# Keeping split weights in a scratch for the second half, in a kernel of one core

## The chip, the cores and the metric

The kernel runs on one core of a Trainium2 chip. The metric is the device time of one execution in microseconds, as the median of several runs. The profile comes from one further execution of the same program.

## The reference

One layer of a hybrid decoder on x of 2048 tokens by 1024, in float32:

```
h = rmsnorm(x, g_pre) * (1 + scale) + shift          # scale, shift, gate from c @ w_ada + b_ada
p = h @ w_in                                         # 1024 x 8704
y_pool = pool_mixer(a_in) * silu(a_g)                # windowed means
y_hgrn = hgrn2_mixer(b_q, b_f, b_i) * silu(b_g)      # gated linear recurrence
y_conv = short_conv_mixer(c_x, c_b, c_c) * silu(c_g) # three taps
y_diff = diff_attention(d_q, d_k, d_v) * silu(d_g)   # 4 heads, two maps each, causal
merged = sum over b of sigmoid(m_g[b]) * (y_b @ w_merge_b)
out = x + gate * rmsnorm(merged @ w_out, g_post)
```

## The kernel before, in words

**Products.** A float32 product is made of three float32r matmuls: each operand is split into a high part (its rounding) and a low part (the rest), and high by high, low by high and high by low are added in PSUM. The projection h @ w_in is done in two halves of 1024 tokens, each with 34 units of 256 output columns (`PAIR_COLS`). A unit is one 2 by 2 block product, and is computed with 7 block products instead of 8 (a Winograd scheme): `PRODUCTS` = 7 x 68 = 476, of which 238 belong to each half. A product is 4 blocks of depth (`KH`) by 3 matmuls of 128x512, 12 matmuls. The 7 left operands of a unit are weights w and sums of weights s; the 7 right ones are blocks of h and their sums t1 to t4.

**Slots.** Every engine runs its own instruction stream, written out by hand as a loop over slots n = 0 to 485. In slot n TensorE does product n into bank gb[n % 2]. ScalarE copies product n-1 out (`copy_out`, L918) or VectorE adds it to an output (`add_out`, L1207). ScalarE rounds the weights of product n+3 (`high`, L902), VectorE makes their low part (`low`, L1197), and GpSimd makes the four sums of weights of the next unit (L753 to L765). The split weights lie in a ring of four (`RING`), three ahead of use (`LEAD`). SyncE issues every DMA, in order, among them two 512 KB loads of weights for each unit (L366, L371). So each weight block is loaded, summed and split twice, once for each half of the tokens.

**The start.** TensorE transposes the 16 blocks of x of the first half into five banks. VectorE and ScalarE evict them as h (`evict`, L1238 and L962). Then ScalarE rounds the seven right operands (`high_h`, L975), and VectorE (operands 0, 2, 3, 6) and GpSimd (1, 4, 5, and the sum t3) make the low parts (`low_h` L1263, `low` L774). The right operands of the second half are kept in a scratch, loaded from slot 230 on and split in slots 233 to 242 (`CHANGE`).

**Attention and mixers** are laid into the slots beside the products. Attention of the first half of the tokens runs over slots 50 to 109, that of the second half over slots 284 to 354. A step of it on TensorE is `attention_ahead` (scores, L1694) and `attention_behind` (the turned-back output L1726, the product with v L1720, the transposes of the probabilities L1708). ScalarE does the exponentials (L988), VectorE the maxima (L1290), the combination (L1322) and the normalised output `on` (L1327). The mixers work in 16 blocks of 128 tokens, eight per half, with bases 12 or 12.5 slots apart from slots 130 and 372 on (`MIX_BASE`). A block's steps have offsets from -17 to +15 against its base, `mix_step(n, offset)`. Three consecutive blocks overlap.

**The end.** When the trunk is over, a second block of instructions, `merge_and_output`, multiplies by the merge weights and w_out.

## Time and profile before

| | |
|---|---|
| median of 3 runs | 2574.45 us (2573.1 to 2575.48) |
| the profiled execution's own time | 2568.26 us |
| its span | 2566.5 us |
| TensorE (matmul) busy | 2284.2 us, 89% |
| VectorE busy | 1689.7 us, 66% |
| ScalarE busy | 1259.9 us, 49% |
| GpSimd busy | 1093.9 us, 43% |
| mean granted TensorE clock | 0.962 |
| DMA | 350.85 MB, mean 137 GB/s |

The span runs from the first to the last instruction of the profiled execution. Busy shares are averages over stages that differ. The stages, as times from the start of the span, are: start to 62 us, then the products of the first half to 1012 us (plain to 236, with attention to about 600, with mixers to 960), those of the second half to 2065 us (plain to 1130, attention to about 1600, mixers after it), and the merge to the end. Matmuls are pipelined, so a busy TensorE is not a TensorE at its peak, and idle time of another engine costs nothing by itself.

### The profile page before, as it was taken

What the parts mean: (1) busy time and instruction counts of PE and PEld (TensorE: products, weight loads), DVE (VectorE), ACT (ScalarE), POOL (GpSimd) and SP (SyncE); (2) the same over time, 40 slices, a digit from 0 to 9 for tenths busy, and PEclk for the clock granted to TensorE, in tenths of its full rate; (3) what the DMA queues carried; (4) which work ended last, traced back from release to release, by engine and by line L of the source; (5) the groups of instructions that cost most, each with busy time, mean ns of one, the idle gap of its engine ahead of it and who ended that gap; (6) DMA issues with size and microseconds to landing.
All of it is one profiled execution on the core that took longest, in us unless ns stands there. A gap on an engine that the chain in (4) does not pass through costs nothing. (4 is left out here: it accounts for less than half of the span.)

```text
span 2566.5 us, 35701 instructions
## 1 busy us (share of the span) xinstructions
PE 2284.2 (89%) x11572; PEld 1859.2 (72%) x11572; DVE 1689.7 (66%) x2872; ACT 1259.9 (49%) x2634; POOL 1093.9 (43%) x883
## 2 busy tenths in 40 slices
PE   3599999999989999998999999999999965989898
PEld 2487777777767777776887888777777744767676
DVE  6776666658888785547777777588888735344442
ACT  3454555535554545445666666445555343434341
POOL 1513323225664654323334333366566425243343
PEclk6799999999999999999999999999999988999999
DMA  6467544334433436453424242343343266576582
GB/s 224 142 201 226 152 131 130 111 96 140 124 112 110 124 103 202 135 155 95 129 79 118 80 117 63 117 128 113 111 129 111 93 213 184 148 208 175 154 223 63
DMA packets 351328, 350.85 MB, mean 137 GB/s; under 512 B 25904, under 2 KB 277168, under 8 KB 350128
## 3 DMA queue, kind: packets, MB, share of 16 engines
q1 hardware_dynamic: 351152, 348.66, 46.0%
q8 instruction: 91, 1.49, 0.3%
q14 instruction: 85, 0.70, 0.1%
HBM read 242.15 MB, written 106.43 MB: 136 GB/s over the span
## 5 line engine op out<-in xcount | busy, mean ns | idle before, releaser
L1622 PE MATMUL gb<-h_hi,w_hi 128*128 128x512 f32 x1904 | 785.8, 413 | 89.1 <-DVE o L1207 53.5
L1624 PE MATMUL gb<-h_hi,w_lo 128*128 128x512 f32 x1904 | 756.3, 397 | 0.0
L1623 PE MATMUL gb<-h_lo,w_hi 128*128 128x512 f32 x1904 | 754.2, 396 | 0.0
L1197 DVE TENSOR_TENSOR w_lo<-w,w_hi 128x512 fp32r<-128x512 f32 x340 | 304.7, 898 | 298.9 <-ACT w_hi L902 298.0
L1622 PEld LDWEIGHTS gb<-h_hi,w_hi 128*128 128x128 f32 x1904 | 365.5, 192 | 175.6 <-issue 98.6
L1624 PEld LDWEIGHTS gb<-h_hi,w_lo 128*128 128x128 f32 x1904 | 364.1, 191 | 80.5
L1623 PEld LDWEIGHTS gb<-h_lo,w_hi 128*128 128x128 f32 x1904 | 366.0, 192 | 66.5
L988 ACT ACTIVATE C_prob<-C_sc,C_negm 128x512 f32<-128x512 f32 (+3 forms) x320 | 198.8, 623 | 270.4 <-DVE C_negm L1290 269.0
L781 POOL TENSOR_TENSOR C_prob<-C_prob,C_cf 128x512 f32<-128x512 f32 (+3 forms) x160 | 161.3, 1027 | 344.3 <-DVE C_cf L1312 330.0
L918 ACT ACTIVATE o<-gb 128x512 f32<-128x512 f32 x272 | 161.3, 593 | 268.5 <-PE gb L1624 255.5
L902 ACT ACTIVATE w_hi<-w 128x512 fp32r<-128x512 f32 x340 | 212.0, 625 | 100.1 <-PE gb L1624 98.9
L765 POOL TENSOR_TENSOR w<-w,s 128x512 f32<-128x512 f32 x68 | 91.1, 1339 | 287.0 <-DVE w_lo L1197 286.4
L753 POOL TENSOR_TENSOR s<-w 128x512 f32<-128x512 f32 x68 | 97.9, 1439 | 264.7 <-DMA w<-in_w_in_dram 251.7
L1207 DVE TENSOR_TENSOR o<-gb,o 128x512 f32<-128x512 f32 x204 | 139.8, 685 | 77.8 <-PE gb L1624 77.5
L1197 DVE TENSOR_TENSOR w_lo<-s,w_hi 128x512 fp32r<-128x512 f32 x136 | 117.2, 862 | 104.5 <-ACT w_hi L902 104.2
L1290 DVE TENSOR_REDUCE C_negm<-C_sc 128x1 f32<-128x512 f32 (+3 forms) x320 | 179.7, 601 | 4.7 <-PE C_sc L1697 2.7
L2168 PE MATMUL D_mb<-D_y_hi,D_wm_hi 128*128 128x512 f32 x320 | 131.2, 410 | 50.7 <-DVE D_gate L2041 31.3
L2000 POOL TENSOR_TENSOR D_gate<-D_gate 128x1024 f32<-128x1024 f32 x32 | 98.1, 3066 | 158.3 <-DVE D_gate L2041 158.3
L1694 PE MATMUL C_sc<-C_ks,C_qt 128*128 128x512 f32 (+3 forms) x320 | 123.2, 385 | 32.2 <-ACT C_prob L988 23.9
L1720 PE MATMUL C_ob<-C_v_tok,C_at 128*128 128x128 f32 x1088 | 149.3, 276 | 1.1 <-ACT C_at L1001 1.1
L1720 PEld LDWEIGHTS C_ob<-C_v_tok,C_at 128*128 128x128 f32 x1088 | 139.3, 191 | 12.9 <-ACT C_at L1001 6.8
L1322 DVE SCALAR_TENSOR_TENSOR C_prob<-C_prob,C_cf 128x512 f32<-128x512 f32 (+3 forms) x160 | 144.5, 903 | 2.6 <-POOL C_prob L781 2.2
(231 smaller groups left out, 4118.2 us busy)
## 6 DMA issues: line engine op xcount, KB each, us to landing
w<-in_w_in_dram SPq DMA_DIRECT2D x136, 512.0 KB, 4.1
gT_scratch<-o SPq DMA_DIRECT2D x128, 256.0 KB, 2.8
D_gate<-gT_scratch SPq DMA_DIRECT2D x32, 1024.0 KB, 9.8
pT_scratch<-o SPq DMA_DIRECT2D x80, 256.0 KB, 2.9
C_qt<-qB_scratch SPq DMA_DIRECT2D x128, 128.0 KB, 2.9
C_ks<-kT_scratch SPq DMA_DIRECT2D x48, 256.0 KB, 4.8
A_x_all<-in_x_dram SPq DMA_DIRECT2D x16, 512.0 KB, 6.9
A_ada<-in_w_ada_dram SPq DMA_DIRECT2D x8, 1024.0 KB, 12.1
```

The costliest lines, as they stand in the source:

```text
L781: tt(second, second, cf[i % 3][:, 1, p:p + 1].to_broadcast([P, width(z)]), ALU.mult).then_inc(scaled, 1)
L902: a(w_hi[n % RING][:, :, :], source(n), ACT.Copy).then_inc(whi, 1)
L918: a(o[b][:, :], gb[n % 2][:, :], ACT.Copy).then_inc(copied, 1)
L988: a(prob[z % PROBS][:, m, 0:width(z)], sc[(2 * z + m) % 3][:, 0:width(z)], ACT.Exp, bias=negm[i % 2][:, m, p:p + 1], accum_out=sums[i % 2] ...
L1197: tt(w_lo[n % RING][:, :, :], source(n), w_hi[n % RING][:, :, :].bitcast(F32), ALU.subtract).then_inc(wlo, 1)
L1207: tt(o[b][:, :], gb[n % 2][:, :], o[c][:, :], ALU.add).then_inc(summed, 1)
L1290: nc.vector.tensor_reduce(negm[i % 2][:, m, p:p + 1], sc[(2 * z + m) % 3][:, 0:width(z)], AX.X, ALU.max, negate=True).then_inc(max_ready, 1)
L1322: stt(first_map, first_map, cf[i % 3][:, 0, p:p + 1], prob[z % PROBS][:, 1, 0:width(z)], ALU.mult, ALU.add).then_inc(a_ready, 1)
L1622: mm(to, hi[:, k, :], h_hi[j][:, k, :], start=(fresh and k == 0), stop=False, skip_group_check=True)
L1623: mm(to, hi[:, k, :], h_lo[j][:, k, :], start=False, stop=False, skip_group_check=True)
L1624: last = mm(to, lo[:, k, :], h_hi[j][:, k, :], start=False, stop=(k == KH - 1), skip_group_check=True)
L1720: last = mm(ob[i % 2][:, 0, :], at[z % 2][:, y, :], v_tok[:, 4 * p + y, :], start=(z == begin[i] and y == 0), stop=(p == 0 and y == nb - 1))
```

## The change

In the first half ScalarE, besides splitting the weights of each product, stores both parts (high and low, now one tensor `w_both` of 512 KB) to a DRAM scratch `wS`: `store_weights(n)`, issued from ScalarE's own DMA queue, two slots ahead of the product, after VectorE has made the low part. `high` waits for the store that last read its place in the ring. For the second half's 238 products `load_weights(n)` brings both parts back, three slots ahead, in place of the loads of w_in, the sums by GpSimd, `high` and `low`. TensorE waits for that load.

In the start the evictions are shared anew: ScalarE takes blocks 0 to 3 and 8 to 15, VectorE 4 to 7. All low parts and t3 of the first half are made by VectorE, with operand 5 ahead of 4.

The mixers' steps are placed anew: ScalarE's `sigmoids` is cut in three (`pool_sigmoid`, `sigmoids`, `affine` a slot later), `distances_x` in two steps each, `decays_first` in two, and several steps are one slot later. In the first half's attention `turn_back` is put behind `values` and `turn`.

The diff, cut to its core ("..." marks lines left out; the arithmetic of counts for the new order is left out whole):

```
@@ -139,8 +148,8 @@
...
-        w_hi = [sb(f"w_hi{j}", [P, KH, P], F32R) for j in range(RING)]
-        w_lo = [sb(f"w_lo{j}", [P, KH, P], F32R) for j in range(RING)]
+        w_both = [sb(f"w_both{j}", [P, 2, KH, P], F32R) for j in range(RING)]
+        w_hi, w_lo = [b[:, 0, :, :] for b in w_both], [b[:, 1, :, :] for b in w_both]
@@ -241,6 +250,9 @@
...
+        w_kept = [sem(f"w_kept{j}") for j in range(RING)]
+        KEEPS = [len(range(r, KEPT, RING)) for r in range(RING)]
@@ -624,9 +652,9 @@
...
-                if j == 1 and u + 1 < UNITS:
+                if j == 1 and u + 1 < NU:
                     load_w1(u + 1)
-                if j == 4 and u + 2 < UNITS:
+                if j == 4 and u + 2 < NU:
                     load_w2(u + 2)
@@ -837,19 +865,10 @@
...
-            for kk in range(2):
-                low(1, kk, 0, operand_part(1, kk))
-            for kk in range(2):
-                t3(0, kk)
-            for j in LOW_BY_POOL[1:]:
-                for kk in range(2):
-                    if j == 4:
-                        pool.wait_ge(t3_made, kk + 1)
-                    low(j, kk, 0, operand_part(j, kk))
...
-                if u + 1 < UNITS:
+                if u + 1 < NU:
@@ -893,6 +912,7 @@
...
                     act.wait_ge(product_done, n - RING + 1)
+                    act.wait_ge(w_kept[n % RING], 16 * (n // RING))
@@ -900,6 +920,17 @@
...
+            def store_weights(n):
+                act.wait_ge(wlo, n + 1)
+                act.dma_start(wS[n], w_both[n % RING][:, :, :, :].bitcast(F32).rearrange("p l k c -> p (l k c)")).then_inc(w_kept[n % RING], 16)
+            def load_weights(n):
+                act.wait_ge(product_done, n - RING + 1)
+                if n < KEPT + RING:
+                    act.wait_ge(w_kept[n % RING], 16 * KEEPS[n % RING])
+                act.dma_start(w_both[n % RING][:, :, :, :].bitcast(F32).rearrange("p l k c -> p (l k c)"), wS[n - KEPT]).then_inc(w_kept[n % RING], 16)
@@ -1034,11 +1060,18 @@
                     act.wait_ge(r_done, 4 * i - 4)
                     act.wait_ge(kt_ready, i - 1)
                 a(f_s[:, :, :], in3[i % 2][:, 2:4, :], ACT.Sigmoid)
-                link(a(k_s[i % 2][:, :, :], in3[i % 2][:, 2:4, :], ACT.Sigmoid, scale=-1.0))
+                a(k_s[i % 2][:, :, :], in3[i % 2][:, 2:4, :], ACT.Sigmoid, scale=-1.0)
+                link(a(q_s[i % 2][:, :, :], in3[i % 2][:, 0:2, :], ACT.Sigmoid))
+            def affine(i):
                 for t in range(2):
                     a(f_s[:, t, :], f_s[:, t, :], ACT.Identity, scale=omlb[:, t:t + 1], bias=lb[:, t:t + 1])
-                    a(k_s[i % 2][:, t, :], k_s[i % 2][:, t, :], ACT.Copy, scale=omlb[:, t:t + 1])
-                a(q_s[i % 2][:, :, :], in3[i % 2][:, 0:2, :], ACT.Sigmoid).then_inc(sig_ready, 1)
+                for t in range(2):
+                    ins = a(k_s[i % 2][:, t, :], k_s[i % 2][:, t, :], ACT.Copy, scale=omlb[:, t:t + 1])
+                ins.then_inc(sig_ready, 1)
+            def pool_sigmoid(i):
                 act.wait_ge(a_loaded, 32 * (i + 1))
                 if i >= 2:
                     act.wait_ge(yp_ready, i - 1)
@@ -1087,26 +1120,32 @@
                 root_x(0, t)
             for n in range(LEAD):
                 high(n)
-            for kk in range(2):
-                high_h(0, kk)
-            for q in range(4, 8):
+            act.wait_ge(mod_ready, 1)
+            for q in range(4):
                 evict(0, q)
-            for kk in range(2):
-                high_h(1, kk)
-            for q in range(12, 16):
+            for j in range(2):
+                for kk in range(2):
+                    high_h(j, kk)
+            for q in range(8, 16):
                 evict(0, q)
             for kk in range(2):
                 high_h(2, kk)
+            for n in range(LEAD - 1):
+                store_weights(n)
             for n in range(SLOTS):
                 u, j = divmod(n, PER)
                 if n and n - 1 < PRODUCTS and (n - 1) % PER in COPIED:
                     copy_out(n - 1)
-                if n + LEAD < PRODUCTS:
+                if n + LEAD - 1 < KEPT:
+                    store_weights(n + LEAD - 1)
+                if n + LEAD < KEPT:
                     high(n + LEAD)
+                elif n + LEAD < PRODUCTS:
+                    load_weights(n + LEAD)
                 if n < 4:
                     for kk in range(2):
-                        high_h(3 + n, kk)
+                        high_h(FIRST_ORDER[3 + n], kk)
                 for b, off in OUT_SLOT.items():
                     for late in range(2):
                         v, r = divmod(n - off - late, PER)
@@ -1168,11 +1211,11 @@
...
-                for t, off in enumerate((-5, -2)):
+                for t, off in enumerate((-5, -1)):
...
-                i = mix_step(n, -1)
+                i = mix_step(n, 0)
@@ -1246,20 +1288,24 @@
...
+            def t3_first(kk):
...
+                tt(parts(h12, kk), parts(h22, kk), parts(h12, kk), ALU.subtract).then_inc(t3_made, 1)
@@ -1359,15 +1405,18 @@
...
-            def distances_x(i, t):
+            def distances_x(i, t, y0, y1):
...
-                for y, m in enumerate(LEVELS):
+                for y in range(y0, y1):
+                    m = LEVELS[y]
...
+                if y1 < NL - 1:
+                    return
@@ -1381,10 +1430,12 @@
...
-            def decays_first(i):
+            def decay_first_queries(i):
...
+            def decay_first_keys(i):
@@ -1457,12 +1508,11 @@
...
-            for q in range(4):
+            for q in range(4, 8):
...
-            for kk in range(2):
-                low_h(0, kk, 0, operand_part(0, kk))
-            for q in range(8, 12):
-                evict(0, q)
+            for j in range(2):
+                for kk in range(2):
+                    low_h(j, kk, 0, operand_part(j, kk))
@@ -1473,17 +1523,18 @@
             for n in range(SLOTS):
                 if n and n - 1 < PRODUCTS and (n - 1) % PER in SUMMED:
                     add_out(n - 1)
-                if n + LEAD < PRODUCTS:
+                if n + LEAD < KEPT:
                     low(n + LEAD)
                 if n == 0:
                     for kk in range(2):
-                        low_h(3, kk, 0, operand_part(3, kk))
-                if n == 1:
+                        t3_first(kk)
+                if n == 2:
                     for kk in range(2):
                         t4(0, kk)
-                if n == 3:
+                if n < 4:
+                    j = FIRST_ORDER[3 + n]
                     for kk in range(2):
-                        low_h(6, kk, 0, operand_part(6, kk))
+                        low_h(j, kk, 0, operand_part(j, kk))
                 for b, off in OUT_SLOT.items():
                     v, r = divmod(n - off, PER)
                     if r == 0 and 0 <= v < UNITS and kind(v) in ("q", "k", "gate"):
@@ -1566,26 +1617,35 @@
                 i = mix_step(n, -8)
                 if i is not None:
                     scan(i)
+                i = mix_step(n, -7)
+                if i is not None:
+                    distances_x(i, 0, 0, 3)
                 i = mix_step(n, -6)
                 if i is not None:
-                    distances_x(i, 0)
+                    distances_x(i, 0, 3, NL - 1)
                 i = mix_step(n, -5)
                 if i is not None:
                     decay_keys(i)
                 i = mix_step(n, -4)
                 if i is not None:
-                    decays_first(i)
+                    decay_first_queries(i)
                 i = mix_step(n, -3)
                 if i is not None:
-                    distances_x(i, 1)
-                i = mix_step(n, 10)
+                    decay_first_keys(i)
+                    distances_x(i, 1, 0, 2)
+                i = mix_step(n, -2)
+                if i is not None:
+                    distances_x(i, 1, 2, NL - 1)
+                i = mix_step(n, 11)
                 if i is not None:
                     advance_state(i)
+                i = mix_step(n, 12)
+                if i is not None:
                     pool_out(i)
                 i = mix_step(n, 14)
                 if i is not None:
                     finish(i)
-                i = mix_step(n, 0)
+                i = mix_step(n, 1)
                 if i is not None:
                     decay_queries(i)
@@ -1604,15 +1664,15 @@
...
-                else:
...
+                pe.wait_ge(*lo_count(half, j, 1))
...
-                    pe.wait_ge(wlo, n + 1)
+                    if n < KEPT:
+                        pe.wait_ge(wlo, n + 1)
+                    else:
+                        pe.wait_ge(w_kept[n % RING], 16 * (KEEPS[n % RING] + (n - KEPT) // RING + 1))
@@ -1734,15 +1788,15 @@
                     turn_back(i)
             def attention_behind(half, s):
-                i = None if half else finished(half, s, ON)
-                if i is not None:
-                    turn_back(i)
                 z = piece(half, s, VALUES)
                 if z is not None:
                     values(z)
                 z = piece(half, s, TURN)
                 if z is not None:
                     turn(z)
+                i = None if half else finished(half, s, ON)
+                if i is not None:
+                    turn_back(i)
             def rounds(i, r):
                 if r == 0:
@@ -2228,10 +2282,11 @@
...
+    wS = nc.dram_tensor("wS_scratch", [KEPT, P, 2 * KH * P], F32).ap()
```

## Rows read from the trace of the kernel before

**Rows 1.** Windows by stage: busy us and (instructions), then granted clock, DMA share, GB/s.
```profile
62.00:140.00 78.00, 50.75 (x202) 40.47 (x202) 62.23 (x64) 41.64 (x69) 36.97 (x16) 0.82 0.42 140
...
140.00:236.00 96.00, 91.64 (x436) 74.94 (x435) 68.87 (x79) 42.98 (x76) 29.78 (x18) 0.96 0.65 215
...
236.00:490.00 254.00, 232.06 (x1227) 192.60 (x1226) 164.33 (x384) 139.57 (x414) 78.32 (x72) 0.99 0.51 144
...
600.00:960.00 360.00, 333.08 (x1828) 265.35 (x1828) 295.50 (x510) 185.80 (x333) 221.55 (x219) 0.97 0.38 116
...
960.00:1012.00 52.00, 50.38 (x240) 41.04 (x238) 28.70 (x40) 23.59 (x36) 17.26 (x10) 1.00 0.58 182
...
1012.00:1130.00 118.00, 110.87 (x494) 90.51 (x495) 59.48 (x72) 55.35 (x92) 44.80 (x28) 0.99 0.46 144
...
1130.00:1600.00 470.00, 438.28 (x2502) 368.52 (x2501) 347.08 (x709) 285.14 (x813) 168.84 (x147) 1.00 0.37 105
...
1600.00:2065.00 465.00, 441.88 (x2361) 354.80 (x2359) 354.99 (x615) 228.93 (x430) 256.38 (x245) 0.98 0.37 112
...
2065.00:2566.00 501.00, 416.68 (x1730) 332.06 (x1728) 206.99 (x249) 185.23 (x217) 200.66 (x88) 0.94 0.63 174
```

**Rows 2.** Windows of L1622 alone, four matmuls to a product.
```profile
140.00:236.00 96.00, 46.54 (x113) 21.71 (x113) 0.96 0.65 215
...
1012.00:1130.00 118.00, 61.72 (x154) 29.37 (x155) 0.99 0.46 144
```

**Rows 3.** Waits of TensorE, 62 to 140 us: total, times, longest us.
```profile
PE gb L1622 <- DVE o L1207: 15.2, 3, 9.8
...
PE gb L1622 <- DVE h_lo L1263: 10.1, 1, 10.1
```

**Rows 4.** Timeline of VectorE in the start: start us, us, instruction.
```profile
57.67 2.36 DVE L1263 TENSOR_TENSOR h_lo<-A_h,h_hi 128x1024 fp32r<-128x1024 f32 x2 [1.12 <-ACT h_hi L975]
...
63.07 6.12 DVE L1246 TENSOR_TENSOR A_h<-A_x_all,A_h 128x1024 f32<-128x1024 f32 x2
```

**Rows 5.** Waits of TensorE, 236 to 600 us.
```profile
PE C_ob L1726 <- DVE C_on L1327: 25.2, 28, 2.5
```

**Rows 6.** Waits of TensorE, 600 to 960 us.
```profile
PE gb L1622 <- DVE o L1207: 14.4, 8, 3.0
...
PE gb L1622 <- ACT o L918: 13.5, 5, 5.6
```

**Rows 7.** Waits of TensorE, 1012 to 1130 us.
```profile
PE gb L1622 <- DVE o L1207: 6.6, 2, 4.4
```

**Rows 8.** Waits of matmuls and of weight loads, 1130 to 1600 us.
```profile
PE C_sc L1694 <- ACT C_prob L988: 23.0, 34, 1.7
...
PEld C_sc L1694 <- ACT C_prob L988: 39.9, 53, 2.1
```

**Rows 9.** Waits of matmuls and of weight loads, 1600 to 2065 us.
```profile
PE gb L1622 <- DVE o L1207: 13.0, 9, 3.0
...
PE gb L1622 <- ACT o L918: 4.9, 4, 2.1
...
PEld gb L1622 <- DVE w_lo L1197: 6.9, 4, 3.1
```

**Rows 10.** Groups of 1012 to 2065 us: busy us, mean ns, idle before, releaser.
```profile
L1197 DVE TENSOR_TENSOR w_lo<-w,w_hi 128x512 fp32r<-128x512 f32 x168 | 150.4, 897 | 156.8 <-ACT w_hi L902 156.2
...
L902 ACT ACTIVATE w_hi<-w 128x512 fp32r<-128x512 f32 x168 | 104.9, 626 | 46.1 <-PE gb L1624 46.1
...
L753 POOL TENSOR_TENSOR s<-w 128x512 f32<-128x512 f32 x33 | 48.4, 1468 | 94.8 <-DMA w<-in_w_in_dram 92.0 <-DVE w_lo L1197 2.8
```

**Rows 11.** Line 421, stores of 512 KB: issue time on SyncE in ns, landing.
```profile
L421 SPq DMA_DIRECT2D hT_scratch<-A_h x8: 319/386/500, 153.3 to 214.1; - x8
...
DMA to landing us min/median/max: 2.6/3.9/5.4
```

**Rows 12.** Transfers, 62 to 140 us in 40 slices: GB/s.
```profile
GB/s 0 0 0 8 0 0 4 0 0 0 0 212 57 4 0 0 0 0 0 4 263 42 273 252 374 418 418 420 401 392 388 338 269 120 307 170 32 237 0 214
```

More of the change, by code:

```diff
@@ L863, in _ @@
                         for kk in range(2):
-                            low(jj, kk, 1, stage[(2 * jj + kk) % STAGES])
+                            low(jj, kk, stage[(2 * jj + kk) % STAGES])
                 for half, s in att_slot(n):
@@ L1237, in evict @@
                     dve.wait_ge(h_hi_ready, 2 * PER)
-                ts((h11 if q < 8 else h12)[:, k, :], tp[q % 5][:, :], gs[:, k:k + 1], mod[:, k:k + 1], ALU.mult, ALU.add).then_inc(h_by_v, 1)
+                ts(rows_of_h(q), tp[q % 5][:, :], gs[:, k:k + 1], mod[:, k:k + 1], ALU.mult, ALU.add).then_inc(h_by_v, 1)
             def t1(half, kk):
-                dve.wait_ge(h_by_v, 8 * half + 8)
+                dve.wait_ge(*evicted(half, 11))
                 if half:
@@ L1745, in attention_behind @@
                     turn(z)
+                i = None if half else finished(half, s, ON)
+                if i is not None:
+                    turn_back(i)
             def rounds(i, r):
```

89 lines of the change are left out of this document (48 added, 41 removed).

## The prediction

> **What bounds the kernel now.** I read the windows by stage first [rows 1]. TensorE is busy for 89% of the whole span, and in the trunk the other engines are well below it: from 236 to 490 us it is busy 232 of 254 us, VectorE 164, ScalarE 140, GpSimd 78. The trunk therefore ends when TensorE has done its products and what lies between them. A product without company takes about 3.06 us: in 118 us there are 154 matmuls of L1622, four to a product, 38.5 products [rows 2]. So time can be won only where TensorE stands still, or runs at a low clock, and I read its own waits next, stage by stage [rows 3, 5 to 9]. The reader is to see that no wait is long, and that in each stage another engine ends it. In the start it is VectorE (15.2 and 10.1 us). In the first half's attention it is the normalised output `on` (25.2 us in 28 waits). In the mixers it is the freeing of a product bank by VectorE or ScalarE (14.4 and 13.5 us, then 13.0 and 4.9). In the second half's attention it is ScalarE's exponential (23.0 us by the matmuls, 39.9 by the weight loads that go ahead of them; the true loss lies between). In the mixers VectorE is busy 295 of 360 us, in the second ones 355 of 465 [rows 1]. The merge, 501 us, is not changed and keeps its time.
>
> **What the second half loses in work.** 238 splits go away. VectorE: 168 of w at 897 ns are 150 us; with the 70 of sums, which have the same shape, 238 x 0.9 = 213 us of its 762 in the three windows from 1012 to 2065 us [rows 1, 10]. ScalarE: 238 x 0.63 = 149 us of 569. GpSimd: four sums for each of 34 units, 136 x 1.47 = 200 us of 470. None of that is TensorE's time, so its worth is what of TensorE's waits it explains.
>
> In attention (1130 to 1600 us) the exponential of a step waits for a maximum, and the maximum stands behind `low`, which waits for `high`, which waits for the product before: 156 us of VectorE's idle time stand before that one line and end with `high` [rows 10]. With both gone the chain of a slot is 0.6 + 0.9 = 1.5 us shorter, and the mean wait is 23.0/34 = 0.7 us, the longest 2.1 [rows 8]. So nearly all go: I take 25 us, from a range of 10 (only half of the 23.0) to 40 (all that the weight loads show).
>
> In the second mixers VectorE falls from 76% to about 355 - 113 = 242 of 465 us, 52% (some 126 of the splits lie there, slots 350 to 475). The bank waits, 13.0 + 4.9 us, and the waits for `low` itself, 6.9 us [rows 9], have little cause left: 18 us of 24.8, between 10 and 25. Where the operands are changed (1012 to 1130 us), 5 of the 6.6 us [rows 7].
>
> **What turn_back behind values and turn is worth.** L1726 waits 28 times for `on`, 0.9 us in the mean and 2.5 at most [rows 5]. It moves behind up to eight products with v and four transposes, which TensorE can do meanwhile because their operands were made a step earlier. They take roughly 1 us. What is late next would be VectorE's `gate_out`, which comes one step later and stands behind it by half a product. I take 20 of the 25.2 us; the ends are 8 and 25.
>
> **The start.** GpSimd leaves it. The two pairs of rows of VectorE show what its company costs: a 128x1024 operation takes 1.18 us alone and 3.06 us beside GpSimd's [rows 4]. Placed by hand, with 1.2 us for each such operation, the low part of operand 2 is ready some 8 us earlier than now, but VectorE then has six more operations of 1.2 us in slots 0 and 1 and four in slot 2, so that products 3 and 4 still wait. Of the 15.2 + 10.1 us of waits [rows 3] I take 10 away, with ends of 0 and 20. The Trainium skill (SBUF — State Buffer, on the shared port pair) says that the second of two such operations blocks fully until the first is done; by that rule VectorE's operations here would each wait out a whole one of GpSimd, and the start would give the upper end, 20. The rows do show more than a doubling, but I keep the 10, because the number of VectorE's operations grows too.
>
> **The mixers of the first half.** VectorE keeps its whole work and it is only spread: waits of 27.9 us [rows 6], each at most 3.0 for VectorE and 5.6 for ScalarE. The cut of `sigmoids` takes four operations out of ScalarE's fullest slot, in which it also does the gate, the convolution's sigmoid and the root of the block before; some of its five waits could go. GpSimd's `decays_second` moves with the rest. I take 12 away, between -5 (a step that is now later is needed sooner, `advance_state` in slot 11 with `norms` in 12) and 22.
>
> **Clock.** In both mixer stages the granted clock is 0.97 and 0.98 of full, in attention 1.00 [rows 1]. It falls to the lower of its two levels, 1.2 GHz, after TensorE has stood still. That costs 0.03 x 360 + 0.02 x 465 = 20 us; with half the waits gone I take 10 back, between 0 and 15.
>
> **What it adds.** First bytes: a store of 512 KB for each of 238 slots, and a load of 512 KB for each of the other 238, less 68 loads. From 140 to 236 us the kernel moves 215 GB/s, and a slot takes 96/28.25 = 3.40 us [rows 1, 2], so that 0.524 MB per slot add 154 GB/s: 369 GB/s. The highest tenths of a stretch with only large transfers are 401 to 420 GB/s [rows 12]. It just fits, with nothing to spare, as from 960 to 1012 us (182 + 0.524/3.06 = 353). I take 5 us for the first and 2 for the second, between 0 and 25. The Trainium skill (DMA: Bandwidth & Descriptors, "Where 436 GB/s comes from") puts what a core gets from HBM at about 358 GB/s; as an estimate by that page the 35.4 MB of this stretch would take 99 us instead of 96, and I would write 3 to 8 instead of 5. No row before has writes and reads at such a rate together.
>
> Then latency. A store is issued in ScalarE's slot n-2 and `high` of the next user waits for it in slot n+1, three slots later. Stores of this size land in 2.6 to 5.4 us, 3.9 in the middle [rows 11]; three slots are 10 us, three plain ones 9.2. A load has three slots less what ScalarE is behind. Both fit; this is cover, and if landing took over 9 us each slot would be paced by it.
>
> Then ScalarE's time: an issue takes SyncE 0.32 to 0.50 us, 0.39 in the middle [rows 11]. On ScalarE that is 238 x 0.39 = 93 us in the first half, where it is busy little more than half [rows 1], and as much in the second, in place of 149. `store_weights` also waits for `low`, so that ScalarE can't run further ahead of VectorE than a slot; `copy_out`, `high` and the exponentials stand behind it. I take 6 us, between 0 and 30. The Trainium skill (DMA: Bandwidth & Descriptors, the table of the fixed cost) gives some 50 ns for the sequencer's part, an estimate of 12 us instead of 93 on ScalarE, and then I would write 2 instead of 6.
>
> **The sum.** -20 (turn_back) -10 (start) -12 (first mixers) -5 -25 -18 (second half) -10 (clock) +7 (bandwidth) +6 (ScalarE) = -87 us. Against the profiled execution's 2568.3 us this is 2481. The median of the runs is 6.2 us above that execution, so the predicted time is 2487 us, 3.4% faster. Changes within 0.2%, 5 us, can't be told from none here.
>
> **The rivals.**
> A. *More is won.* If the second half's attention and mixers give their upper ends (40 + 25) and the start 20, the sum is -87 - 15 - 7 - 10 = -119: 2455 us. For it: every engine but TensorE is relieved at once. Against: when one wait goes, the next engine's is a few tenths of a us behind.
> B. *The traffic eats half of it.* In the plain stretches the ring is at the DMA engines' rate; loads by SyncE that share the 16 engines come later too, and GpSimd's sums with them. With bandwidth and ScalarE at their upper ends (+25, +30) and the second half at -30 instead of -48: -87 + 18 + 24 + 18 = -27, and half of that mishap -57: 2517 to 2547 us.
> C. *Slower: stores pace the first half.* One mechanism: if a store beside all other traffic lands so late that `high` waits, then a slot lasts a third of the landing time. The first half has 238 slots in 950 us, 4.0 us each, the plain ones 3.1 to 3.4. Let 165 slots be shorter than 4 us, 3.5 in the mean (an estimate between 3.4 and 4.0). Landing in 12 us makes them 4.0, +82 us, which the gains of 100 still carry; in 13 us 4.33, +137: from there it decides, and at 14 us (+193) the time is 2574 - 100 + 6 + 193 = 2673 us. For it: the 369 GB/s above. Against: the 2.6 to 5.4 us of the same size in that very stretch [rows 11]. The same page's 358 GB/s is the rule that would bring it about, if backlog grew there; by my count it grows by 3 us only.
> D. *Nothing changes*: gains and costs cancel, or TensorE's waits are only renamed since products themselves set the pace. The rows with waits speak against it.
>
> **Chances.** The forecast, 2462 to 2512 us, 0.50. A, below it, 0.15. B, 2512 to 2560, 0.22. D 0.03. C 0.10. Faster by over 0.2%: 0.50 + 0.15 + 0.22 = 0.87; same 0.03; slower 0.10. The range that leaves out no more than 2 in 10 goes from 2445 (all but the best of A) to 2550 (most of B).
>
> **What would show it.** In the profile after: no L902, L1197 and L753 to L765 in the second half; VectorE at 55 to 60% there; the wait of L1694 for the exponential under 10 us; L1726's wait for `on` under 8 us; products' waits for `w_both` loads near nothing, and `high` waiting for a DMA hardly at all. The second half lasts about 1000 us instead of 1053 (-48 and half of the clock's 10), the first about 30 less. The prediction fails if ScalarE's line 902 waits for stores, if L1622 waits for loads, or if the first half's slots from 140 to 236 us grow over 3.7 us.

## The result, and the profile after

The changed kernel takes 2536.5 us (median of 4, 2534.6 to 2538.1) against 2575.0 us for the kernel before beside it: a ratio of 0.985, 95% interval 0.9833 to 0.9867. It is 38 us faster, where 87 were forecast. The time lies inside the range, in what rival B gave. The two profiled executions are 33 us apart (2568.3 and 2534.9 us), since that of before was 6.7 us under its median, so what is read below from the profiles adds up to some 5 us less than the medians show. One execution of e8 below took 2864.7 us at a granted clock of 0.76, and e8's median is of its other three.

From the page of the changed kernel, the span, part 1 and the line of packets:

```profile
span 2533.1 us, 35157 instructions
...
PE 2274.4 (90%) x11572; PEld 1871.5 (74%) x11572; DVE 1434.6 (57%) x2638; ACT 1144.1 (45%) x2400; POOL 839.4 (33%) x739
...
DMA packets 383963, 564.75 MB, mean 223 GB/s; under 512 B 32432, under 2 KB 248880, under 8 KB 382768
```

VectorE has lost 255 us of work, ScalarE 116 and GpSimd 254 (213, 149 and 200 were worked out for the second half alone), and the chip moves 565 MB instead of 351. The windows of the changed kernel are cut near the places where products 0, 42, 110, 238, 284 and 355 begin and the last one ends, and the last window is the merge (columns as in [rows 1]):

```profile
62.00:237.00 175.00, 140.81 (x619) 113.21 (x618) 119.41 (x145) 83.41 (x141) 42.23 (x26) 0.89 0.86 311
237.00:567.00 330.00, 293.33 (x1537) 245.32 (x1536) 200.21 (x461) 171.60 (x504) 94.52 (x87) 0.97 0.71 234
567.00:1050.00 483.00, 439.00 (x2256) 350.68 (x2255) 348.65 (x588) 231.51 (x405) 243.18 (x242) 0.95 0.73 255
1050.00:1192.00 142.00, 130.76 (x586) 106.73 (x585) 29.06 (x40) 38.44 (x61) 9.47 (x4) 0.99 0.90 281
1192.00:1632.00 440.00, 436.73 (x2596) 382.76 (x2596) 296.03 (x664) 261.04 (x769) 114.78 (x112) 0.99 0.54 166
1632.00:2032.00 400.00, 397.87 (x2174) 322.25 (x2172) 197.56 (x455) 149.47 (x267) 128.51 (x169) 1.00 0.76 239
2032.00:2533.00 501.00, 417.17 (x1728) 332.62 (x1728) 207.13 (x249) 184.50 (x216) 200.70 (x88) 0.94 0.64 174
```

The DMA share of the plain part of the first half is 0.86, where the stretches of [rows 1] had 0.42 and 0.65. The starts of products, read off the timeline of the first matmul line, show where the time went (us from the start of the span, and the difference to before):

| product | before | after | difference |
|---|---|---|---|
| 7 | 110.6 | 100.8 | -9.8 |
| 14 | 136.7 | 133.0 | -3.7 |
| 42 | 232.7 | 236.5 | +3.8 |
| 60 | 305.4 | 317.2 | +11.8 |
| 110 | 553.9 | 566.7 | +12.8 |
| 130 | 612.3 | 632.7 | +20.4 |
| 238 | 1012.7 | 1050.0 | +37.4 |
| 284 | 1152.8 | 1191.5 | +38.7 |
| 300 | 1268.6 | 1294.4 | +25.8 |
| 355 | 1635.2 | 1632.2 | -3.0 |
| 475 | 2062.3 | 2028.5 | -33.9 |

The start won its 10 us. From product 7 to 238 the first half then lost 47 us. The second half won 71, all of it after product 284. So two large terms stand against each other. The waits of TensorE say the same. First half of the changed kernel (62 to 1050 us), the bank waits of the kernel before over its first half (62 to 1013 us), then the second half of the changed kernel (1050 to 2032):

```profile
PE gb L1682 <- DVE o L1250: 37.9, 11, 10.0
PE gb L1682 <- ACT o L949: 31.6, 10, 8.3
PE C_ob L1774 <- DVE C_y_out L1380: 17.5, 13, 2.9
PE C_sc L1748 <- DVE C_causal_r L1330: 10.6, 1, 10.6
PE C_ob L1780 <- DVE C_on L1373: 7.9, 10, 2.3
```

```profile
PE gb L1622 <- DVE o L1207: 36.2, 13, 9.8
...
PE gb L1622 <- ACT o L918: 14.0, 6, 5.6
```

```profile
PE gb L1682 <- ACT o L949: 10.0, 4, 5.5
PE gb L1682 <- DMA w_both<-wS_scratch: 2.2, 2, 1.9
PE C_sc L1748 <- ACT C_prob L1014: 2.1, 4, 0.8
```

In the second half the 23.0 us for the exponential [rows 8] are 2.1, the 13.0 for VectorE [rows 9] are gone, and the loads from the scratch cost 2.2. In the first half the waits for a bank that VectorE frees are as they were, 36.2 and 37.9 us, and those for a bank that ScalarE frees have grown from 14.0 to 31.6. The wait for `causal_r` is 10.6 us, and 17.5 us stand before L1774 (the product with v), which had waited for no output of VectorE before. No wait there names a store of weights. From 140 to 236 us a product takes 3.80 us in the mean (3.42 before), over the 3.7 that the prediction named as a sign of failure. The stores show in ScalarE's waits, 62 to 1030 us:

```profile
ACT w_both L922 <- DVE w_both L1240: 76.0, 45, 6.9
...
ACT hb L978 <- DMA vT_scratch<-hb: 9.5, 2, 5.0
ACT o L949 <- DMA gS_scratch<-o: 8.5, 2, 7.3
ACT hb L971 <- DMA kT_scratch<-hb: 7.4, 1, 7.4
```

76 us it stands before `high`, released by `low`: that is `store_weights` waiting for the low part. The others are small stores of SyncE that free `hb` and `o`, and land late. In the kernel before, only 3.6 us of ScalarE's waits in the first half end with such a store. (Waits before `hb` that the view puts down to "issue" come on top, 8.2 us before and 14.0 now; the one below is of these.) One of them can be followed. The DMA row and the rates of 95 to 130 us in 40 slices:

```profile
DMA  9999999999999999999999999999999998999999
GB/s 400 391 236 220 332 379 286 290 351 431 407 417 421 426 426 412 417 421 417 431 412 421 391 391 371 393 402 426 403 272 321 438 411 318 312 363 400 392 380 406
```

The engines are full for 35 us. SyncE has issued eight 512 KB loads of x and one of `w_ada` there, and behind them, at 101.91 us, a 256 KB store of k from `hb`. Its issue takes 0.33 us, but it lands only at 116.42, 14.5 us later, after all of those loads; before, it was 9.2 us. Until then ScalarE may not write that `hb`: it stands for 11.53 us. VectorE's low part of the output stands behind ScalarE (11.46 us), its next `add_out` behind that, and TensorE waits 10.00 us for the bank. The next k store shows the same crowding at the issue, which takes 6.89 us (1.57 us before), but its landing, at 119.21, isn't what ScalarE waited for. From the timelines of SyncE, ScalarE, VectorE and TensorE:

```profile
101.91 0.33 SPq L423 DMA_DIRECT2D kT_scratch<-hb  x1
...
103.75 6.89 SPq L423 DMA_DIRECT2D kT_scratch<-hb  x1
```

```profile
116.50 0.63 ACT L971 ACTIVATE hb<-o 128x512 fp32r<-128x512 f32 x1 [11.53 <-issue]
```

```profile
117.16 0.69 DVE L1263 TENSOR_TENSOR o<-o,hb 128x512 fp32r<-128x512 f32 x1 [11.46 <-ACT hb L971]
...
118.43 0.68 DVE L1250 TENSOR_TENSOR o<-gb,o 128x512 f32<-128x512 f32 x1
```

```profile
119.26 0.77 PE L1682 MATMUL gb<-h_hi,w_both 128*128 128x512 f32 x1 [10.00 <-DVE o L1250]
```

The other mechanism in the same form, as the mixers begin. VectorE waits 7.32 us for the mixers' constants. Its next `low` ends at 590.2. ScalarE, which began to copy a product out at 583.2, can issue the store only at 590.26 and round the next weights at 590.71:

```profile
578.44 0.69 DVE L1240 TENSOR_TENSOR w_both<-w,w_both 128x512 fp32r<-128x512 f32 x1
586.46 0.48 DVE L1384 MEMSET B_AT<- 128x512 f32 x1 [7.32 <-DMA B_yh<-const_inv_first_dram]
...
588.49 1.75 DVE L1240 TENSOR_TENSOR w_both<-w,w_both 128x512 fp32r<-128x512 f32 x1
```

```profile
583.22 0.60 ACT L949 ACTIVATE o<-gb 128x512 f32<-128x512 f32 x1 [1.60 <-PE gb L1684]
590.26 0.33 ACTq L926 DMA_DIRECT2D wS_scratch<-w_both  x1
590.71 0.63 ACT L922 ACTIVATE w_both<-w 128x512 fp32r<-128x512 f32 x1 [6.90 <-DVE w_both L1240]
```

### The profile page after: what moved, and what is told of

It reads as the page before. It is cut to its first block and busy times, and to the rows that moved or that the text cites. A ratio compares the mean times of both kernels' runs of the same rounds, so it can differ in the third digit from the quotient of the medians.

```text
span 2533.1 us, 35157 instructions
## 1 busy us (share of the span) xinstructions
PE 2274.4 (90%) x11572; PEld 1871.5 (74%) x11572; DVE 1434.6 (57%) x2638; ACT 1144.1 (45%) x2400; POOL 839.4 (33%) x739
## 5 line engine op out<-in xcount | busy, mean ns | idle before, releaser
L1682 PE MATMUL gb<-h_hi,w_both 128*128 128x512 f32 x1904 | 789.0, 414 | 87.2 <-ACT o L949 41.7
L1684 PE MATMUL gb<-h_hi,w_both 128*128 128x512 f32 x1904 | 757.7, 398 | 0.0
L1683 PE MATMUL gb<-h_lo,w_both 128*128 128x512 f32 x1904 | 756.7, 397 | 0.0
L1682 PEld LDWEIGHTS gb<-h_hi,w_both 128*128 128x128 f32 x1904 | 366.9, 193 | 171.2 <-issue 91.7
L1684 PEld LDWEIGHTS gb<-h_hi,w_both 128*128 128x128 f32 x1904 | 365.7, 192 | 81.2
L1683 PEld LDWEIGHTS gb<-h_lo,w_both 128*128 128x128 f32 x1904 | 367.7, 193 | 67.1
L1240 DVE TENSOR_TENSOR w_both<-w,w_both 128x512 fp32r<-128x512 f32 x170 | 142.1, 836 | 171.5 <-ACT w_both L922 171.1
L1774 PEld LDWEIGHTS C_ob<-C_v_tok,C_at 128*128 128x128 f32 x1088 | 142.8, 191 | 32.9 <-issue 23.1
L1774 PE MATMUL C_ob<-C_v_tok,C_at 128*128 128x128 f32 x1088 | 148.6, 276 | 17.5 <-DVE C_y_out L1380 17.5
L922 ACT ACTIVATE w_both<-w 128x512 fp32r<-128x512 f32 x170 | 106.8, 628 | 103.2 <-DVE w_both L1240 55.6
L1368 DVE SCALAR_TENSOR_TENSOR C_prob<-C_prob,C_cf 128x512 f32<-128x512 f32 (+3 forms) x160 | 134.2, 840 | 2.3 <-POOL C_prob L809 2.2
L1748 PE MATMUL C_sc<-C_ks,C_qt 128*128 128x512 f32 (+3 forms) x320 | 119.8, 374 | 13.2 <-DVE C_causal_r L1330 10.6
L781 POOL TENSOR_TENSOR s<-w 128x512 f32<-128x512 f32 x34 | 48.3, 1422 | 248.7 <-DMA w<-in_w_in_dram 214.2
L2223 PE MATMUL D_mb<-D_y_lo,D_wm_hi 128*128 128x512 f32 x320 | 128.2, 401 | 0.0
L2224 PE MATMUL D_mb<-D_y_hi,D_wm_lo 128*128 128x512 f32 x320 | 127.8, 399 | 0.0
```

Source lines behind the costliest of these rows:

```text
L1240: tt(w_lo[n % RING][:, :, :], source(n), w_hi[n % RING][:, :, :].bitcast(F32), ALU.subtract).then_inc(wlo, 1)
L1368: stt(first_map, first_map, cf[i % 3][:, 0, p:p + 1], prob[z % PROBS][:, 1, 0:width(z)], ALU.mult, ALU.add).then_inc(a_ready, 1)
L1682: mm(to, hi[:, k, :], h_hi[j][:, k, :], start=(fresh and k == 0), stop=False, skip_group_check=True)
L1683: mm(to, hi[:, k, :], h_lo[j][:, k, :], start=False, stop=False, skip_group_check=True)
L1684: last = mm(to, lo[:, k, :], h_hi[j][:, k, :], start=False, stop=(k == KH - 1), skip_group_check=True)
L1774: last = mm(ob[i % 2][:, 0, :], at[z % 2][:, y, :], v_tok[:, 4 * p + y, :], start=(z == begin[i] and y == 0), stop=(p == 0 and y == nb - 1))
```

## The experiments

All are edits of the changed kernel, and each time is a median of 4 with its ratio to the kernel before, run on the same chip. In e3, e4 and e5 the second half reads the weights of the first four products over and over, so they don't compute the layer, though the second half moves the same bytes.

| run | us | ratio, 95% interval |
|---|---|---|
| e1 turn_back first | 2537.2 | 0.9847 (0.9823 to 0.9872) |
| e2 no keeping | 2554.1 | 0.9908 (0.9884 to 0.9933) |
| e3 tiny stores | 2498.6 | 0.9694 (0.9672 to 0.9717) |
| e4 no stores | 2487.9 | 0.9651 (0.9627 to 0.9674) |
| e5 half stores | 2509.8 | 0.9753 (0.9731 to 0.9775) |
| e6 x loads spread | 2535.2 | 0.9841 (0.9819 to 0.9864) |
| e7 stores by SyncE | 2508.5 | 0.9743 (0.9727 to 0.9759) |
| e8 e6 and e7 | 2509.6 | 0.9738 (0.9716 to 0.9760) |
| e9 keep from product 49 | 2517.9 | 0.9773 (0.9748 to 0.9798) |
| e10 e9 and e7 | 2505.9 | 0.9718 (0.9695 to 0.9741) |
| e11 e7, turn_back first | 2519.2 | 0.9774 (0.9753 to 0.9795) |
| e12 e7, old mixer slots | 2523.5 | 0.9785 (0.9759 to 0.9812) |
| e13 e7, ScalarE waits | 2517.8 | 0.9785 (0.9766 to 0.9805) |
| e14 high before store | 2518.0 | 0.9786 (0.9767 to 0.9805) |

### The stores: bytes, waits, issues (e3, e4, e5)

```
 def store_weights(n):                     # e3; the loads read wS[n % 4]
     act.wait_ge(wlo, n + 1)
-    act.dma_start(wS[n], w_both[n % RING] ...)
+    act.dma_start(wS[n][:, 0:16], w_both[n % RING][:, 0, 0, 0:16] ...)      # from n = 4 on
-if n + LEAD - 1 < KEPT:                   # e4
+if n + LEAD - 1 < 4:
     store_weights(n + LEAD - 1)
+    act.dma_start(wS[n][:, 0:KH * P], w_both[n % RING][:, 0, :, :] ...)     # e5: the high part
```

> The changed kernel, but from product 4 on a store carries 64 bytes of each partition instead of 4 KB, with the same waits and the same issues by ScalarE; the second half loads the first four products' weights over and over, so its results are other ones, its bytes the same. Theory of traffic (stores of SyncE land late behind the weights' stores, and ScalarE waits for them): the first half ends 20 us or more earlier, product 238 at 1030 us or before, the time 2515 or less. Rival of coupling (ScalarE waits for `low` before each store and pays for each issue): the first half ends within 5 us of now, the time is 2530 to 2537.

> The changed kernel with no stores of weights but the first four: neither their traffic, nor their waits, nor their issues; the second half loads the first four products' weights over and over, so its results are other ones, its bytes the same. If the stores as a whole cost the first half about 45 us (37 us later at product 238 although 10 us ahead at product 7), it ends at about 1005 us and the time is 2490. What lies between this and the tiny stores is the coupling and the issues: by the theory of traffic under 8 us, by that of coupling 25 us or more.

> The changed kernel, but a store carries only the high part (2 KB of each partition, 256 KB) from product 4 on; waits and issues as they are. The second half loads the first four products' weights over and over: other results, the same bytes. The full stores cost 38 us more than tiny ones. Theory of saturation (only the stretches in which the 16 DMA engines are full pay: about 95 to 130, 190 to 230 and 245 to 275 us of the changed kernel): with half the bytes these stretches hardly fill, and well under half of the 38 us stays: 2500 to 2510. Rival (each byte stored costs everywhere, because every landing is later): half stays, 2515 to 2520.

Tiny stores take 38 us off (2536.5 to 2498.6); no stores at all take 49. In this order the bytes cost 38 us, and the waits and issues by ScalarE 11. The order matters, as e7 shows below. Product 238 begins at 1014.3 us with tiny stores and 997.5 without, against 1050.0. The 36 us of difference to tiny stores are not spread: 5.6 come between products 7 and 14, 8.1 from 28 to 50, 6.3 from 50 to 60, 7.8 from 110 to 130, 5.9 from 226 to 238, and 0.4 in the 96 products between 130 and 226. The engines are full or nearly so in the first, second and last of these (DMA shares of 1.02, 0.93 and 0.92), and at 0.77 and 0.80 in the other two, against 0.70 in the 96 products without loss. But products 14 to 28 run at 1.02 too and lose nothing (47.1 us before, 47.1 now). So full engines alone cost nothing; in the stand followed above it took a transfer that frees a buffer which ScalarE needs next. The DMA row and rates of 95 to 130 us with tiny stores:

```profile
DMA  9979999999999999999995999607999402692014
GB/s 384 237 211 318 332 300 314 413 412 406 426 411 407 418 402 403 380 393 389 399 337 209 383 187 335 206 10 171 365 278 289 110 0 28 131 403 46 0 9 128
```

Now it is mainly the eight loads of x that fill the engines, and the second half of the stretch has air. With half the bytes 11 of the 38 us stay (2509.8). That is less than half of them, as the theory of saturation has it, although at 2510 it stands at that theory's edge.

Without stores TensorE's waits of 62 to 1000 us are still these:

```profile
PE gb L1682 <- DVE o L1250: 32.8, 15, 4.7
...
PE gb L1682 <- ACT o L949: 12.0, 5, 8.3
```

So some 45 us of waits for a bank are there whatever the stores do, against 50 in the kernel before (36.2 + 14.0).

### Everything but the keeping (e2)

```
-if n + LEAD < KEPT:
-    high(n + LEAD)
-elif n + LEAD < PRODUCTS:
-    load_weights(n + LEAD)
+if n + LEAD < PRODUCTS:
+    high(n + LEAD)        # likewise low, load_w1, load_w2 and the sums; no store_weights
```

> The changed kernel without the keeping of weights: no store, no load from the scratch, every weight loaded, summed and split in both halves as before; the new start, the new mixer slots and the new place of turn_back stay. Theory (those edits give the start's 10 us, take back some 8 at turn_back, and the mixers little): 2560 to 2575. Rival (my prediction's terms: start 10, turn_back 20, first mixers 12, and as much again in the second mixers): 2520 to 2535.

2554.1 us, 21 us less than before: more is gained than the first theory said, and much less than by the rival. By products, 10.1 us are won at product 7, 14.8 at 110 (turn_back's stretch), 9.8 at 238, 13.3 at the end. So from product 110 to 238, where the mixers have their new slots, 5 us are lost (458.7 to 463.7 us). Against e2 the keeping is worth some 15 to 18 us net in the changed kernel (by ratios, and by medians). The second half takes 1049.7 us before, 1046.1 without keeping and 980.2 with it and no stores. The keeping gives 66 us there, and in the plain part of it, products 238 to 284, nothing (142.6 us without, 143.4 with).

### turn_back (e1, e11)

```
+i = None if half else finished(half, s, ON)
+if i is not None:
+    turn_back(i)
 z = piece(half, s, VALUES)
 ...
-i = None if half else finished(half, s, ON)
-if i is not None:
-    turn_back(i)
```

> The changed kernel with turn_back put back ahead of values and turn in the first half's attention, and nothing else. Theory (the wait is only renamed: values of a unit needs y_ready of the unit two before, which VectorE's gate_out gives just ahead of normalise): L1774's wait for y_out (17.5 us) goes, L1780's wait for `on` returns to about 25 us; the time changes by -8 us to 0, 2528 to 2536. Rival (the move is worth the 20 us that I gave it, and other things cost more): 2550 to 2556.

> Stores issued by SyncE, and turn_back ahead of values and turn again. The profiles of the changed kernel with and without the move differ by 5 us in the attention of the first half, their medians by nothing. If the move is worth 5 us: 2512 to 2515. If it only renames the wait: 2507 to 2510.

On the changed kernel the move is worth nothing that the medians show (2537.2 against 2536.5). The wait of the attention stretch (200 to 575 us) goes where the theory said, from L1774's `y_out` back to `on`:

```profile
PE C_ob L1780 <- DVE C_on L1373: 31.7, 28, 3.2
```

31.7 us, against 17.5 + 7.9 = 25.4 with the move. With the stores at SyncE undoing it costs 11 us (2519.2 against 2508.5; the intervals just overlap), more than either expectation. In the attention's own stretch, products 50 to 110, the profiles show 5.7 us (e1) and 5.1 (e11) for it. The rest of e11's loss lies in products 110 to 238, where turn_back has no part, and stays unexplained. Its worth is about 5 us, between 0 and 11, not 20.

### Bursts and units (e6, e8, e9, e10)

```
-if n == PREP:                     # e6
-    for t in range(8): load_x(1, t)
+if 0 <= n - PREP < 8: load_x(1, n - PREP)
-if n + LEAD - 1 < KEPT:           # e9
+if PER * 7 <= n + LEAD - 1 < KEPT:
     store_weights(n + LEAD - 1)
-if n + LEAD < KEPT:
+if n + LEAD < PER * (NU + 7):
     high(n + LEAD)                # likewise low, loads and sums; load_weights after that
```

> The changed kernel with the eight loads of x for the second half (512 KB each) issued one a slot from slot 5 on, where now all eight are issued at slot 5; each is needed four slots later. Theory of saturation: the stand of TensorE for 10.0 us at 119 us, behind a k store that waits behind them, goes: 6 us less at product 14, 2528 to 2532. Rival (the total bytes of the stretch decide, not the burst): the loss only moves to a later product, 2535 to 2538.

> Both: x loads one a slot, and stores issued by SyncE. If each takes its own loss away, their gains add: 2516 to 2522. If SyncE's queue is itself what is late, no better than the spread loads alone, 2530.

> The changed kernel, but the first 7 units (products 0 to 48) are not kept: no stores of them, and the second half loads, sums and splits their weights again (products 238 to 286), as the kernel before does. Theory of saturation: the first 50 products pay 13 us for the traffic, and keeping gains nothing in the plain part of the second half (142.6 us from product 238 to 284 without keeping, 143.4 with it and no stores): 2520 to 2526. Rival (saved work is worth the same in each product, 66 us in 238): 49 of them are worth 14 us, and the time stays at 2535 to 2540.

> The same, with the stores issued by SyncE. Stores by SyncE took 28 us off; of the traffic of the first 50 products some 8 us were left beside them. If the gains are of separate places: 2494 to 2502, the fastest so far. If SyncE's gain was mostly in the first 50 products: 2505 or more.

Spreading the x loads moves the loss: 6.0 us are won at product 14 and 5.5 of them are lost again by product 21. The rival holds, and e8 adds nothing to e7. Not keeping the first 49 products takes 18.6 us off (2517.9), a little more than expected, though 49 of 238 kept products are given up: product 50 begins at 243.2 us instead of 258.3, and the second half's plain part loses nothing. Together with SyncE's stores it is 2505.9 us, the lowest time of the runs that compute the layer, but its interval overlaps that of e7: the second of the two expectations holds, and the gains don't add.

### Who issues the stores (e7, e13, e14) and the mixer slots (e12)

```
+for n in range(SLOTS):            # e7: at the head of SyncE's slot, none on ScalarE
+    if n + LEAD - 1 < KEPT:
+        sp.wait_ge(wlo, n + LEAD)
+        sp.dma_start(wS[n + LEAD - 1], ...)
+if n + LEAD - 1 < KEPT:           # e13: e7, and in ScalarE's slot
+    act.wait_ge(wlo, n + LEAD)
 if n + LEAD < KEPT:               # e14: on the changed kernel
     high(n + LEAD)
+if n + LEAD - 1 < KEPT:           # moved behind high
+    store_weights(n + LEAD - 1)
```

> The changed kernel with the stores of weights issued by SyncE at the head of its slot instead of by ScalarE: the same bytes, but ScalarE neither waits for `low` nor issues. Theory of coupling (no stores against tiny stores: 10.7 us): 2522 to 2528, the gain in slots 100 to 226. Rival (SyncE stands at waits for outputs and the stores come later, so that `high` waits for their landing): 2540 or more, with `w_both` L922 waiting for DMA.

> Stores issued by SyncE as in the fastest so far but one, but ScalarE waits for `low` of product n+2 in slot n, at the place where the store stood, and issues nothing. If that wait is what SyncE's issue takes away (a late VectorE, or a late DMA behind which VectorE stands, then holds copy_out and the exponentials too): 2525 or more. If the issue and the second DMA queue are what costs (ScalarE's stores share the 16 engines with SyncE's smaller ones packet by packet): 2508 to 2514.

> The changed kernel with `high` of product n+3 ahead of the store of n+2 in ScalarE's slot, so that the wait for `low` no longer holds the next rounding, though it still holds what follows. By the theory of the wait: part of the 28 us back, 2520 to 2530. By that of the queue: 2534 to 2538.

> Stores issued by SyncE, and all of the mixers' steps back in their old slots (one piece of sigmoids, distances_x and decays_first each, and the old offsets). My prediction gave the new slots 12 us in the first half and a share in the second. If that holds, 2520 or more. If the new slots are worth nothing beside lighter engines (the profile without keeping shows 5 us lost in the first mixers and 3.5 won in the second half): 2503 to 2512.

SyncE's stores take 28 us off, with every byte still stored, which is more than the 11 us that waits and issues cost when the stores are tiny; neither expectation had it. ScalarE's wait for a landing, the rival's fear, is small (62 to 1030 us):

```profile
ACT w_both L930 <- DMA wS_scratch<-w_both: 6.1, 2, 5.5
```

With the wait alone put back (e13) 9 of the 28 us return; ScalarE's idle time before `high` is again what it was:

```profile
ACT w_both L930 <- DVE w_both L1243: 81.5, 61, 5.8
```

With issue and second queue kept but `high` ahead of the store (e14), 18.5 us are won, and that idle time falls from 76.0 to

```profile
ACT w_both L922 <- DVE w_both L1240: 9.4, 4, 4.3
```

though another 16 us now stand before three later lines of ScalarE.

So neither theory holds alone. Where the time goes can be told by adding up products. The first group has the stretches in which the tiny stores won (products 7 to 60, 110 to 130, 226 to 238), the second the others (60 to 110, 130 to 226), in us:

| | first group | second group |
|---|---|---|
| kernel before | 288.9 | 613.2 |
| e4 no stores | 288.3 | 608.6 |
| e3 tiny stores | 288.5 | 624.7 |
| changed kernel | 322.1 | 627.1 |
| e7 stores by SyncE | 309.4 | 610.1 |
| e13 e7, ScalarE waits | 309.0 | 618.9 |
| e14 high before store | 316.7 | 615.6 |

The bytes cost 34 us in the first group and 2 in the second (e3 to the changed kernel). ScalarE's waits and issues cost 16 us in the second and nothing in the first (e4 to e3). e7 takes away all of the second cost, and 13 us of the first. The wait alone is 9 us of the second group (e7 to e13). What is left between e13 and the changed kernel, 13 us and 8, belongs to the issue at that place or to the second queue, and no run separates them.

What e7 does not take away is as telling. It is 21 us slower than e4 (2508.5 against 2487.9), and ScalarE still waits 32 us for small stores of SyncE there (32 in the changed kernel, 4 in e3 and e4). So their late landing goes with the 21 us that the traffic costs whoever issues the stores; it can't be what e7 won.

The old mixer slots cost 15 us (2523.5 against 2508.5), 9 of them by product 238. So beside the stores the new slots are worth about what I gave them. Without stores they are not: products 110 to 238 take 463.7 us in e2 and 459.3 in e4, against 458.7 before.

## Why the prediction was wrong

The direction and the rival's range hold. The sum of the gains came out near its size, but by luck, and the costs were far too small.

**Second half, 48 us and 5 of the clock: 71 measured**, 66 by the keeping (e4 against e2 by products). The chain was right: with `high` and `low` gone the exponential's wait fell to 2 us. The size was a quarter too small, and most of that is attention: products 284 to 355 take 440.6 us instead of 482.4, 42 us less where 25 were forecast. TensorE's idle time there fell from 32.4 us to 3.3, and its busy time for the same matmuls by 12.7 though the clock was no higher, so the 39.9 us of waits that the weight loads showed [rows 8] were the better measure than the matmuls' 23.0. The mixers after it gave 31 us for 18 and the clock: nearly every stand of TensorE ended, and the granted clock went from 0.98 to 1.00. Where the operands are changed nothing was won (140.2 to 141.5 us, 5 forecast). The prediction also gave VectorE's 156 us of idle time to attention, while [rows 10] covers the whole second half.

**Start, 10: right**, 9.8 us at product 7. Product 2 began 5.7 us earlier (82.2 to 76.6), where I had placed its operand 8 earlier. VectorE's sums that took 3.06 us each beside GpSimd's operations take 1.18 without them (63.16 us):

```profile
63.16 2.36 DVE L1288 TENSOR_TENSOR A_h<-A_x_all,A_h 128x1024 f32<-128x1024 f32 x2 [0.31 <-ACT A_x_all L992]
```

**turn_back, 20: about 5. The step that failed is the sentence that its followers' operands were made a step earlier.** `values` of a unit's first piece also waits for `y_ready` of the unit two before (`if z == begin[i] and i >= 2`), which `gate_out` gives just ahead of `normalise` on VectorE. So the 25.2 us [rows 5] became 17.5 + 7.9. I had read what is late next as `gate_out`, but not who waits for it.

**First mixers, 12: not there against the kernel before**, where e2 loses 5 us in products 110 to 238 and e4 0.6. The new slots only keep off 10 us of what the stores by SyncE would cost there (e12). And the clock's 10 came in the second half alone: in products 130 to 226 the granted clock fell from 0.97 to 0.95.

**What it adds, bandwidth 7 (0 to 25) and ScalarE's time 6 (0 to 30): 49 measured. These are the terms that made the prediction wrong.** How the 49 us divide depends on what is taken away first. With ScalarE issuing, the bytes are 38 and the waits and issues 11 (e3, e4). With SyncE issuing, the bytes are 21 (e7 against e4), and 28 are ScalarE's part, 9 of them the wait (e13). In the first order bandwidth was outside its bounds; in the second each term is inside them, near its upper end, and the failure is that both came nearly whole.

The sum of rates was right: 369 GB/s were worked out, and full stretches run at 400 to 430. What failed is the step from "it just fits" to a price. I set the landing of the weights' own stores (4.4 us now) against three slots of cover, and that cover held: TensorE and `high` never waited for them. I did not ask who else is on the engines. The small stores of SyncE that free `o` and `hb` have less: the outputs of slots 6 and 8 of a unit, two slots apart, share one `hb`. In the first half these stores land in 7.0, 7.7 and 6.3 us (medians of eight each), where it was 5.6, 3.5 and 2.9. The changed kernel from 62 to 1050 us, then the kernel before from 62 to 1013:

```profile
wS_scratch<-w_both ACTq DMA_DIRECT2D x238, 512.0 KB, 4.4
...
kT_scratch<-hb SPq DMA_DIRECT2D x8, 256.0 KB, 7.0
...
vT_scratch<-hb SPq DMA_DIRECT2D x8, 256.0 KB, 7.7
gS_scratch<-o SPq DMA_DIRECT2D x8, 256.0 KB, 6.3
```

```profile
kT_scratch<-hb SPq DMA_DIRECT2D x8, 256.0 KB, 5.6
...
vT_scratch<-hb SPq DMA_DIRECT2D x8, 256.0 KB, 3.5
gS_scratch<-o SPq DMA_DIRECT2D x8, 256.0 KB, 2.9
```

ScalarE stands in order behind them (11.5, 7.4, 7.3 us), and TensorE behind ScalarE's copies or VectorE's sums. That the loads come in bursts is not the reason: spread out they cost the same (e6). The Trainium skill (DMA: Bandwidth & Descriptors, "Issuing engines are not separate DMA queues") says that DMAs of all engines run on the same 16 DMA engines and interleave; the landings above agree with it, and it would have pointed at this victim. The Trainium skill's 358 GB/s from HBM (the same page, "Where 436 GB/s comes from"), weighed in the prediction, is not a ceiling here: 35 us at 378 GB/s in the mean, with stores and loads together.

For ScalarE's time I had named the wait for `low` and what stands behind it, and priced it at next to nothing. An issue takes 0.33 us there, near the 0.39 of the first working and not the 50 ns of the other.

In the sum: gains of 100 forecast, 87 measured (e4, 2487.9 us); costs of 13 forecast, 49 measured. That the changed kernel without its stores takes what I predicted with them is chance. In the profile of e4 the second half gives 70 us instead of 48 and the clock's 10, and turn_back and the first mixers together 5 instead of 32. Rival B came true by its first half, full engines and ScalarE's part, while its other half, a second half worth only 30 us, is refuted. Rival C did not come near: landings are 4.4 us, not 13.

## What to carry to other kernels

When a change fills the DMA engines, don't only ask whether the new transfers have cover: list the small old ones that share the engines, what buffer each frees, and how many slots it has. Price the traffic and its issuing engine together, since each can cost more beside the other (e3, e4, e7). Give up the kept work where engines are full and its saving is nothing (e9), and keep an issue with its wait off the engine whose next operation paces the pipeline, or behind that operation (e7, e14). When a wait is moved behind two others, read every semaphore of those two before calling it hidden.

## What the runs showed of the hardware

An issue on ScalarE's DMA queue takes 0.33 us (median of 476, 0.78 at most); SyncE's 1159 issues take 0.44 in the median. An issue can take far longer in a full stretch: 6.89 us for a store behind eight loads of x, where the same store took 1.57 us before and 1.70 in e4, and 4.34 in e7. Whether the full engines or what SyncE's own queue already held made it long isn't settled.

Two queues share the engines. The eight loads of x landed some 1.3 us apart in the kernel before. In the changed kernel four of them (103.2 to 110.5 us) landed 1.9 to 2.6 us apart, while ScalarE's stores were in flight, and the last two 1.3 us apart again. What SyncE issued behind them, small stores too, landed after them.

A stretch can run at a DMA share of 0.90 (1050 to 1192 us, loads from the scratch) with only 2.2 us of TensorE's waits for these loads. But it wins nothing from the work that was taken out of it: 9.1 us of waits for a bank of ScalarE's stand there (2.7 before), and ScalarE waits 27 us for small stores of SyncE, one of them for 14.0 us (6.3 before in all). These two lines are of the changed kernel, 1050 to 1192 us:

```profile
PE gb L1682 <- ACT o L949: 9.1, 3, 5.5
```

```profile
ACT o L949 <- DMA gS_scratch<-o: 14.0, 1, 14.0
```
